# Router logits and the first pair's gather placed between the halves of the output projection, on rows before their norm

## The chip, the cores and the metric

One core of a Trainium2 chip. The metric is device time in microseconds (us) of one execution; lower is better. The engines are TensorE (PE; its weight loads are listed as PEld), VectorE (DVE), ScalarE (ACT), GpSimd (POOL) and SyncE (SP), which here only issues transfers. POOL issues transfers too.

## The reference, cut to what matters

One decoder layer for 320 tokens: a prompt of 256 and 8 sequences of 8 new tokens ("the sample"). Two recurrent mixers, a gated merge, an output projection, then a mixture of 32 experts of which each token takes 4:

```python
merged = sigmoid(gate_a) * (o_a @ w_up_a) + sigmoid(gate_b) * (o_b @ w_up_b)
x = x + merged @ w_o
h2 = _rms(x, norm2_w)                       # x * rsqrt(mean(x*x) + eps) * norm2_w
logits = h2 @ w_router + b_router
top_v, top_e = top_k(logits, 4)
gates = softmax(top_v)
# each chosen expert e: (clip(up) + 1) * swish(min(gate, 7)) @ w_down[e], weighted by its gate
x = x + sum over the four experts
y = _rms(x, norm_f_w)
```

All is float32. An expert has 8 MB of gate and up weights and 4 MB of down weights; all 32 are read, 403 MB.

## The kernel before, in words

Tokens lie in three tiles: tile 0 and tile 1 are the prompt's 128 rows each, tile 2 the sample's 64, kept as 128 half rows of 512 columns (`xs`). `TILE_ORDER` is 2, 0, 1.

**The ring.** `ring` has 12 slots of 1 MB. In the layer, five slots take the panels of the input and up projections in turn (`MIX`), and the four after them (5 to 8) the output matrix `w_o` (`WO`, L432); `merged`, the input of the output projection, lies in the ring behind these (L173). In the expert loop the ring is six chunks of 2 MB (`chunk`): four of gate and up weights, two of down weights. It thus holds one expert. SP loads chunks 1 and 0 of expert 0 when the last up projections are done (L438) and chunks 2 to 5 when the last product with `w_o`, named `wo11`, is (L441). After that, `load_expert` (L447) fetches chunk c of the next expert as soon as TensorE has used chunk c of this one.

**Order of work.** Each engine runs its own list, written out by hand; engines meet at semaphores. The eight PSUM banks are handed out by a list of names, `psum_order`: the i-th name gets bank i mod 8. `take` waits until the bank's last user has emptied it, `done` signals that it is full, `free` that it is emptied.

**The stretch of the change** on TensorE (L1000 to L1133): product `wo2` (sample tile; L628), `wo00` (tile 0, left half of the columns; L967), the sum of squares of the sample (L1010), `wo01`, the turning of the gate and up biases (L1015), the turning of the sample's normed rows `h2s` (L978), `wo10` (tile 1), the sample's logits (L998), `wo11`, then turning (L983) and logits (L998) of tile 0 and tile 1, then for each tile the slot of every token in its experts (`place`, L1034 and L1037: running counts by a triangular matmul), the counts (L1062), the gather of the rows of the first two experts (`gather_part`, L1047: a one-hot matrix `Psel` times `h2`), its turning (`turn_tokens`, L1054), the turning of the gates (L1129), the reading of the loop count, and the loop, which begins with `gate_up` (L628).

DVE adds the products to the residual rows (L1770, L1801), scales them by the inverse root and the norm weights (`norm_rows`, L1779, L1782), finds the four best experts (`top4`, L1787 to L1793: one compare and add for each of the four), turns slots into one-hot matrices (L1817, L1818, L1827), and computes counts (L1832 to L1836) and gates (L1839, L1841). ACT squares rows for the norm (L1189, L1381), evicts turned rows (L1389, L1393), takes the exponentials (L1396, L1397), and evicts gathered and turned tokens (L1422, L1426). POOL loads the norm weights when the last up projection is done (L537 to L542), six transfers that `s_late` counts with two of bias matrices, and TensorE waits for `s_late` ahead of the biases' turn.

The loop takes two experts in a turn and gathers the rows of the next two meanwhile.

Of the kernel before, what the change touches and what calls it, by code (L numbers as in the profile page):

```python
# [16 lines left out]
ALU = mybir.AluOpType  # L17
ACT = mybir.ActivationFunctionType
AX_X = mybir.AxisListType.X

D = 1024
# [41 lines left out]

def psum_order():
# [34 lines left out]
    o += ["wo2", "wo00", "x2s", "wo01", "bgu", "hT2", "wo10", "lg2", "wo11", "hT00", "hT01", "lg0", "hT10", "hT11", "lg1"]  # L99
    o += [f"sl{s}" for s in TILE_ORDER] + ["cnt", "wT"]  # L100
# [3 lines left out]
PSUM_USE = {name: (i % 8, i // 8) for i, name in enumerate(psum_order())}  # L104


def build(nc, x_prompt, x_sample, state_gdn, state_gdn_conv, state_gla, norm1_w, w_in, conv_w, a_log, dt_bias,
# [3 lines left out]
    with ExitStack() as ctx:  # L111
# [61 lines left out]
        merged = flat(ring, (MIX + WO) * 2048, (KD, TOK))  # L173
        gate_b23 = flat(ring, W1 + 3072, (2, TOK))
# [27 lines left out]
        rows = sb("rows", [64, 128])  # L202
        cols = sb("cols", [128, 64])
# [26 lines left out]
        slot1 = sb("slot1", [128, 3, EXPERTS])  # L230
# [20 lines left out]
        iota = sb("iota", [128, SLOTS])  # L251

# [40 lines left out]
        s_cst, xl_ready, xg2_ready, gbr_ready = sem("cst_in"), sem("xl_ready"), sem("xg2_ready"), sem("gbr_ready")  # L293
# [97 lines left out]

        def chunk(c):
            return ring[:, 4096 * c:4096 * c + 4096]
# [5 lines left out]
        def _(sp):  # L399
# [7 lines left out]
            sp.dma_start(rows[58:60, :], gla_gk_b[0].rearrange("(k p) -> k p", p=128)).then_inc(s_rows, 16)  # L407
            sp.dma_start(cst_rows, state_gdn_conv[0].rearrange("b w c -> (b w) c")).then_inc(s_cst, 16)
# [61 lines left out]
        def _(pool):  # L470
# [27 lines left out]
            for g in range(2, 4):  # L498
# [5 lines left out]
                           allow_small_or_imprecise_dtypes=True))  # L504
            step(pool.memset(ab[:, :, :], 0.0), consts)
# [7 lines left out]

            freed(pool, "tail2")
# [31 lines left out]
            step(pool.memset(y_sl, 0.0))  # L546
            step(pool.memset(GTs, 0.0), gtr_done)
# [3 lines left out]
        def _(pe):  # L551
# [30 lines left out]
            for s in range(3):  # L582
                if s == 1:
                    pe.wait_ge(s_rows, 16 * 5)
                    o = take("cols")
                    done(pe.transpose(o[:, 0:60], rows[0:60, :], ident[0:60, 0:60]), "cols")
# [375 lines left out]
            def wo(s, f):  # L962
                n, a = TILE_N[s], TILE_0[s]
                o = take(f"wo{s}{f}")
                for k in range(KD):
                    c = D * (k % 2) + 512 * f
                    mm = pe.matmul(o[0:n, :], merged[:, k, a:a + n], slot(MIX + k // 2)[:, c:c + 512],  # L967
                                   start=(k == 0), stop=(k == KD - 1))
                done(mm, f"wo{s}{f}")

            def turn_h2(s):

                n = TILE_N[s]
                pe.wait_ge(h2_ready, 1 + TILE_ORDER.index(s))
                if s == 2:
                    o = p3(take("hT2"), 4, 128)
                    for k in range(4):
                        mm = pe.transpose(o[:, k, :], h2s[:, 128 * k:128 * k + 128], ident[:, :])  # L978
                    done(mm, "hT2")
                for f in range(2 if s < 2 else 0):  # L980
                    o = p3(take(f"hT{s}{f}"), 4, 128)
                    for k in range(4):
                        mm = pe.transpose(o[:, k, 0:n], h2[0:n, s, 512 * f + 128 * k:512 * f + 128 * k + 128],  # L983
                                          ident[0:n, 0:n])
                    done(mm, f"hT{s}{f}")

            def logits(s):

                n, a = TILE_N[s], TILE_0[s]
                if s < 2:  # L990
                    freed(pe, f"hT{s}1")
                    freed(pe, f"hT{s}0")
                else:
                    freed(pe, "hT2")
                o = take(f"lg{s}")
                for k in range(KD):
# [3 lines left out]
                done(mm, f"lg{s}")  # L1000

            o = take("wo2")
            for k in range(KD):
                mm = halves(o, merged[:, k, PROMPT:TOK], slot(MIX + k // 2)[:, D * (k % 2):D * (k % 2) + D], k == 0,
                            k == KD - 1)
            done(mm, "wo2")
            wo(0, 0)
            pe.wait_ge(x2_sum, 1)
            o = take("x2s")
            done(pe.matmul(o[:, 0:1], pairs[:, :], ss[:, 5:6], start=True, stop=True), "x2s")  # L1010
            wo(0, 1)
            pe.wait_ge(s_late, 128)
            o = take("bgu")
            for j in range(4):
                mm = pe.transpose(o[:, 128 * j:128 * j + 128], b_raw[:, j:512:4], ident[:, :])  # L1015
            done(mm, "bgu")
            turn_h2(2)
            wo(1, 0)
            pe.wait_ge(s_misc, 64)
            logits(2)  # L1020
            wo(1, 1)
            turn_h2(0)
            logits(0)
            turn_h2(1)
            logits(1)

            def place(s):
# [10 lines left out]
                done(mm, f"sl{s}")  # L1038

# [16 lines left out]

            place(2)
            place(0)
            place(1)
            o = take("cnt")  # L1060
            for i, s in enumerate(TILE_ORDER):
                mm = pe.matmul(o[:, 0:EXPERTS], ones[0:TILE_N[s], :], msk[0:TILE_N[s], s, :], start=(i == 0), stop=(i == 2))  # L1062
            done(mm, "cnt")
# [44 lines left out]
            def emptied(banks):  # L1108

                for b in banks:  # L1110
                    pe.wait_ge(pfree[b], max(u for nm, (bb, u) in PSUM_USE.items() if bb == b and nm != "wT") + 1)
# [12 lines left out]
            pe.wait_ge(gate_ready, 3)  # L1124
            assert PSUM_USE["wT"][0] not in (0, 1, 6, 7)
            o = take("wT")
            for s in range(3):
                n, a = TILE_N[s], TILE_0[s]
                mm = pe.transpose(o[0:EXPERTS, a:a + n], gate_all[0:n, s, 0:EXPERTS], ident[0:n, 0:n])  # L1129
            done(mm, "wT")  # L1130
# [804 lines left out]
```

## Time and profile before

| | |
|---|---|
| median of 3 runs | 1383.34 us (1382.59 to 1384.22) |
| profiled execution, its own time | 1385.51 us |
| its span, first to last instruction | 1383.4 us |
| TensorE busy | 1300.4 us, 94% of the span |
| DVE, ACT, POOL busy | 433.2, 296.3, 32.4 us |
| mean granted TensorE clock | 0.983 |
| bytes moved by transfers | 447.71 MB, mean 324 GB/s |

Times in rows are microseconds from the span's start, "mean ns" is one instruction's duration, x the number of instructions, and L12 is line 12 of the kernel. What stands after an arrow `<-` in a wait is what ended it. A granted clock of 1.00 is 2.4 GHz, 0.50 is 1.2 GHz. Matmuls are pipelined, so that their durations overlap; the pace is read from starts, or from the chain of waits.

### The profile page before, as it was taken

Reading aid. Unit: us, or ns where it says so; the run is one execution under the profiler, and the core shown is the slowest. Engines: PE = TensorE matmul, PEld = TensorE weight load, DVE = VectorE, ACT = ScalarE, POOL = GpSimd, SP = SyncE. Lnnn points to the kernel's source line nnn. Section 1 sums busy time; section 2 is a strip of 40 time slices with the busy share of each in tenths; the row PEclk is TensorE's granted clock in tenths of the full one; section 3 lists DMA queues with packets and bytes.
Section 4 is the critical chain, followed back from the end, with each engine's and each line's share of the span. In section 5 each row is a group of like instructions: output and inputs, shape, how many; then the busy total and the mean of one; then the engine's idle time right before and its main releaser. Section 6 shows DMA issues by size and latency. Waiting matters only on the chain.

```text
span 1383.4 us, 15693 instructions
## 1 busy us (share of the span) xinstructions
PE 1300.4 (94%) x5861; PEld 613.2 (44%) x5861; DVE 433.2 (31%) x806; ACT 296.3 (21%) x530; POOL 32.4 (2%) x71
## 2 busy tenths in 40 slices
PE   7999989989999999999999999999999999999996
PEld 5777678746545333333333333333333333333332
DVE  3536566273123231223212133121232212232123
ACT  2374542220022022021120111111021110211102
POOL 5000000001000000000000000000000000000000
PEclk9999989999997999999999999999999999999999
DMA  9522200217536999999999999999999999999993
GB/s 276 170 88 70 92 31 1 69 61 244 198 122 256 417 429 428 428 428 429 428 429 428 429 428 429 428 429 429 429 428 429 428 429 428 428 429 428 429 428 137
DMA packets 61833, 447.71 MB, mean 324 GB/s; under 512 B 7597, under 2 KB 30201, under 8 KB 37228
## 3 DMA queue, kind: packets, MB, share of 16 engines
q1 hardware_dynamic: 59820, 440.34, 77.1%
q0 software_dynamic: 1984, 6.98, 1.5%
q8 instruction: 18, 0.29, 0.1%
q14 instruction: 11, 0.09, 0.0%
HBM read 442.29 MB, written 5.02 MB: 323 GB/s over the span
## 4 chain that ended last, share of the span: by engine, by line
PE 46%; DMA 46%; DVE 5%; ACT 1%; issue 1%; SPq 0%; DVEq 0%; ACTq 0%
DMA ring<-in_w_gate_up_dram 46%; PE bank L628 18%; PE bank L577 14%; PE bank L967 2%; PE bank L1047 2%; PE bank L831 1%; PE bank L642 1%; PE bank L843 1%; PE bank L839 1%; PE bank L998 0%; PE bank L619 0%; PE bank L1054 0%; PE bank L1076 0%; PE bank L677 0%; PE bank L1096 0%
## 5 line engine op out<-in xcount | busy, mean ns | idle before, releaser
L628 PE MATMUL bank<-ring,zgb 128*64 128x512 f32 x2560 | 565.7, 596 | 46.1 <-DMA ring<-in_w_gate_up_dram 36.9
L628 PEld LDWEIGHTS bank<-ring,zgb 128*64 128x64 f32 x2560 | 179.5, 137 | 429.0 <-issue 329.7
L1880 DVE COPY zgb<-bank 128x512 f32<-128x512 f32 x32 | 22.1, 692 | 637.0 <-PE bank L628 637.0
L577 PE MATMUL bank<-hTb,ring 128*128 128x320 f32 x640 | 179.5, 439 | 1.3 <-DVE hTb L1498 1.3
L577 PEld LDWEIGHTS bank<-hTb,ring 128*128 128x128 f32 x640 | 121.9, 192 | 53.8 <-issue 4.7
L628 PE MATMUL bank<-ring,cv 128*64 128x512 f32 x512 | 116.9, 598 | 0.0
L1431 ACT COPY zgb<-bank 128x512 f32<-128x512 f32 x32 | 18.8, 587 | 419.5 <-PE bank L628 419.5
L1047 PE MATMUL bank<-h2b,Sl 128*128 128x512 f32 (+1 forms) x204 | 86.0, 630 | 0.0
L1441 ACT COPY hTb<-bank 64x512 f32<-64x512 f32 x64 | 37.1, 580 | 197.4 <-PE bank L628 196.4
L1076 PE MATMUL bank<-hTb 128*128 128x512 f32 x136 | 68.2, 606 | 0.0
L1855 DVE TENSOR_TENSOR xbuf<-xbuf,bank 128x512 f32<-128x512 f32 x85 | 58.4, 687 | 20.1 <-PE bank L628 11.2
L628 PEld LDWEIGHTS bank<-ring,cv 128*64 128x64 f32 x512 | 33.9, 136 | 58.7 <-issue 54.8
L1096 PEld LDWEIGHTS bank<-ident,zgb 128*128 128x128 f32 x256 | 39.4, 204 | 34.8 <-ACT zgb L1431 19.5
L1047 PEld LDWEIGHTS bank<-h2b,Sl 128*128 128x128 f32 (+1 forms) x204 | 29.8, 197 | 32.6 <-issue 32.5
L1096 PE MATMUL bank<-ident,zgb 128*128 128x128 f32 x256 | 42.3, 288 | 0.0
L1422 ACT COPY h2b<-bank 128x512 f32<-128x512 f32 x34 | 19.9, 586 | 66.7 <-PE bank L1047 66.7
L1426 ACT COPY zgb<-bank 128x512 f32<-128x512 f32 x34 | 19.9, 586 | 58.7 <-PE bank L1054 58.2
L1076 PEld LDWEIGHTS bank<-hTb 128*128 128x128 f32 x136 | 22.3, 193 | 22.9 <-issue 22.9
L1435 ACT ACTIVATE Gc<-qb 128x512 f32<-128x512 f32 x32 | 20.2, 632 | 43.4 <-DVE qb L1891 42.9
L1827 DVE TENSOR_TENSOR Sl<-iota,vTM 128x192 f32<-128x192 f32 x66 | 23.6, 358 | 18.0 <-DVE cv L1896 8.1
L1889 DVE TENSOR_TENSOR qb<-bank,Sg 128x512 f32<-128x512 f32 x32 | 22.1, 692 | 21.7 <-PE bank L1096 18.3
L967 PE MATMUL bank<-ring 128*128 128x512 f32 x64 | 28.4, 597 | 0.0
(388 smaller groups left out, 984.6 us busy)
## 6 DMA issues: line engine op xcount, KB each, us to landing
ring<-in_w_gate_up_dram SPq DMA_DIRECT2D x128, 2048.0 KB, 23.6
ring<-in_w_down_dram SPq DMA_DIRECT2D x64, 2048.0 KB, 20.6
ring<-in_w_in_dram SPq DMA_DIRECT2D x22, 1024.0 KB, 5.2
ring<-in_w_o_dram SPq DMA_DIRECT2D x4, 1024.0 KB, 12.4
ring<-in_w_up_a_dram SPq DMA_DIRECT2D x2, 1024.0 KB, 4.9
ring<-in_w_up_b_dram SPq DMA_DIRECT2D x2, 1024.0 KB, 5.0
out_dram<-Sg POOLq DMA_DIRECT2D x1, 2048.0 KB, 13.1
xbuf<-in_x_prompt_dram SPq DMA_DIRECT2D x2, 512.0 KB, 3.9
```

Of the source, the lines that this page charges most:

```text
L577: mm = pe.matmul(o[0:m, 0:TOK], w[:, k, c0:c0 + m], rhs[:, k, :], start=(k == 0), stop=(k == kk - 1))
L628: mm = pe.matmul(o[64 * f:64 * f + 64, 0:width], lhs, w[f] if isinstance(w, list) else w[:, width * f:width * f + width], start=start, sto ...
L967: mm = pe.matmul(o[0:n, :], merged[:, k, a:a + n], slot(MIX + k // 2)[:, c:c + 512], start=(k == 0), stop=(k == KD - 1))
L1047: return pe.matmul(o[:, :], lhs, rhs, start=(s == TILE_ORDER[0]), stop=(s == TILE_ORDER[-1]))
L1076: mm = pe.matmul(bank[SC[j]][:, :], GTs[:, TILE_0[s]:TILE_0[s] + 128], y_sl[:, 512 * f:512 * f + 512], start=True, stop=True)
L1096: mm = pe.transpose(bank[FMB[q]][:, 128 * j:128 * j + 128], pre[:, q, j:512:4], ident[:, :])
L1435: link(A(sbuf_[:, :, :, :], gbuf[:, :, :, :], ACT.Sigmoid, scale=ALPHA), sg_ready, n * 2 + (x + 1))
L1441: ins = nc.scalar.copy(y_sl[SLOTS * x:SLOTS * x + SLOTS, 512 * f:512 * f + 512], bank[DN[x]][64 * f:64 * f + 64, :])
L1827: return TTo(dst[:, :, SLOTS * x:SLOTS * x + SLOTS], mid(iota[:, :], 3), c, ALU.is_equal)
L1855: link(TTo(v, v, bank[SC[j]][:, :], ALU.add), acc_done, n * 5 + i)
L1880: link(V.tensor_copy(pre[:, 1, :], bank[PRE[1]][:, :]), pre_done[1], n * 2 + (x + 1))
L1889: inner(TTo(dst[:, :, :, :], src, bias, ALU.add))
```

## The change

- **Routing on rows before the norm.** Logits are taken from the residual rows themselves; the router matrix is scaled once by the norm weights (as columns, read with the small rows at the start), and the inverse root comes in when DVE adds the router's bias. The square sums of a prompt tile are taken by halves of its columns.
- **By halves, between the products.** The turning, the logits, the slots and the counts of tiles 2 and 0 stand between the products of the output projection and between the halves of those of tile 1; those of tile 1 as far as its rows are there.
- **The first pair's gather** is made per tile, and turned: the residual rows are the stationary operand and the one-hot matrix, scaled by the inverse root, the moving one. DVE's eviction applies the norm weights. The first `gather_part` and `turn_tokens`, their evictions on ACT and their waits are gone; those in the loop stay, and their semaphore counts shift.
- **`top4`** compares all four experts in one instruction and sums them in a second.
- **The output matrix** goes into the last four slots, `merged` into `h2b` (prompt and sample apart, so two adds); chunk 3 of expert 0 is issued behind the output matrix, chunk 2 with chunks 1 and 0, chunks 4 and 5 behind `wo11`.
- **Moved:** the scaled rows `h2` behind the gates; POOL's clearing of two tiles no longer stands in front of ACT's exponentials; DVE's wait for all output transfers stands ahead of the first product's add.

The diff, cut:

```diff
-        merged = flat(ring, (MIX + WO) * 2048, (KD, TOK))
+        merged = flat(h2b, 0, (2, KD, 128))
+        merged_s = flat(h2b, 2 * D, (KD, 64))
...
+            sp.dma_start(rows[60:68, :], norm2_w[0].rearrange("(k p) -> k p", p=128)).then_inc(s_rows, 16)
...
-                sp.dma_start(slot(MIX + k).rearrange("p (k n) -> p k n", k=2), src).then_inc(wfull[MIX + k], 16)
+                sp.dma_start(wo_slot(k).rearrange("p (k n) -> p k n", k=2), src).then_inc(wfull[MIX + k], 16)
+            sp.dma_start(chunk(3), expert_chunk(0, 3)).then_inc(e_full[3], 16)
...
-                if i % MIX in (3, 0):
-                    c = {3: 1, 0: 0}[i % MIX]
+                if i % MIX in (3, 4, 0):
+                    c = {3: 1, 4: 2, 0: 0}[i % MIX]
...
-            for c in range(2, CHUNKS):
+            for c in range(4, CHUNKS):
...
+            pool.dma_start(n2p[:, :].rearrange("p (k i) -> p k i", i=2), norm2_w[0].rearrange("(k p i) -> p k i", p=128, i=2)
+                           ).then_inc(s_n2p, 16)
...
+            def first_tokens(s, f):
+                o = p3(bank[f], 4, 2 * SLOTS)
+                pe.wait_ge(first_ready, TILE_ORDER.index(s) + 1)
+                for k in range(4):
+                    c = 256 * (k // 2) + k % 2
+                    if s < 2:
+                        lhs, rhs = x_tm[:, s, 512 * f + c:512 * f + c + 255:2], Psel[:, s, :]
...
+            wo_part(0, 0, take("wo00"), range(KD))
+            turn_x2(2, 0)
...
+            wo_part(0, 1, take("wo01"), range(KD))
+            pe.wait_ge(s_late, 128)
...
+            pe.wait_ge(wr_ready, 1)
+            logits_part(2, take("lg2"), range(KD))
+            turn_x2(0, 0)
+            turn_x2(0, 1)
+            o = take("wo10")
+            wo_part(1, 0, o, range(4))
             place(2)
+            lg0 = take("lg0")
+            logits_part(0, lg0, range(4))
+            logits_part(0, lg0, range(4, KD))
+            wo_part(1, 0, o, range(4, KD))
             place(0)
+            cnt = take("cnt")
+            count(2, cnt)
+            count(0, cnt)
+            o = take("wo11")
+            wo_part(1, 1, o, range(4))
+            turn_x2(1, 0)
+            wo_part(1, 1, o, range(4, KD))
+            lg1 = take("lg1")
+            logits_part(1, lg1, range(4))
+            turn_x2(1, 1)
...
+            for f in range(2):
+                first_tokens(2, f)
+            logits_part(1, lg1, range(4, KD))
+            for f in range(2):
+                first_tokens(0, f)
             place(1)
+            done(count(1, cnt), "cnt")
+            for f in range(2):
+                first_tokens(1, f).then_inc(xt_full[f], 1)
+            pe.wait_ge(gate_ready, 3)
...
-            emptied((6, 7))
-            pe.wait_ge(p_ready, 1)
-            for f in range(2):
-                gather_part(f, 2)
-            for f in range(2):
-                gather_part(f, 0)
-                gather_part(f, 1).then_inc(g_full[7 - f], 1)
-            emptied(range(6))
-            for f in range(2):
-                pe.wait_ge(xr_done, f + 1)
-                turn_tokens(f)
...
+                step(TTo(merged_s[:, m, :], ga[:, PROMPT:TOK], gb[:, PROMPT:TOK], ALU.add))
+                step(TTo(merged[:, :, m, :], ga, gb, ALU.add), mrg_ready)
...
+            dve.wait_ge(s_misc, 64)
+            step(TTo(wr[:, :, :], wr[:, :, :], last(cols[:, 60:68], EXPERTS), ALU.mult), wr_ready)
...
+            dve.wait_ge(out_sem, 96)
             o = full(dve, "wo2")
             free(TTo(xs, xs, o[:, :], ALU.add), "wo2")
             add_rows("wo00", 0, 0)
+            inverse_rms(2)
             add_rows("wo01", 0, 1)
+            top4(2)
+            inverse_rms(0)
+            first_slots(2)
+            top4(0)
             add_rows("wo10", 1, 0)
+            first_slots(0)
             add_rows("wo11", 1, 1)
+            o = p3(full(dve, "hT11"), 4, 128)
+            free(V.tensor_copy(hT[:, 4:8, 128:256], o), "hT11")
+            inverse_rms(1)
             top4(1)
+            first_slots(1)
...
+            for f in range(2):
+                dve.wait_ge(xt_full[f], 1)
+                step(TTo(xTe[:, 4 * f:4 * f + 4, :], p3(bank[f], 4, 128), last(n2p[:, 4 * f:4 * f + 4], 128), ALU.mult),
+                     xg_done)
+            dve.wait_ge(s_late, 128)
+            for s in range(3):
+                norm_rows(s)
```

## Rows read from the trace of the kernel before

**Rows 1.** Busy time of each engine by stretch (from:to, length, engines).

```profile
core 0: us, PE busy (x) PEld busy (x) DVE busy (x) ACT busy (x) POOL busy (x), PEclk, DMA share, GB/s
...
360.00:371.00 11.00, 11.00 (x43) 7.75 (x42) 0.49 (x1) 0.87 (x2) 0.00 (x0) 1.00 0.00 0
...
431.00:444.00 13.00, 10.63 (x37) 4.42 (x37) 2.51 (x8) 4.25 (x7) 0.00 (x0) 0.80 0.03 10
...
500.00:1340.00 840.00, 798.58 (x3514) 290.21 (x3512) 206.70 (x362) 128.58 (x214) 0.00 (x0) 1.00 1.01 428
```

**Rows 2.** TensorE's waits over the whole span (us in total, times, longest).

```profile
PE bank L628 <- DMA ring<-in_w_gate_up_dram: 36.9, 38, 1.2
```

**Rows 3.** Timeline of the SP queue's issues (start, us, line, count).

```profile
371.75 0.82 SPq L438 DMA_DIRECT2D ring<-in_w_gate_up_dram  x2
...
410.01 0.81 SPq L441 DMA_DIRECT2D ring<-in_w_gate_up_dram  x2
...
443.79 10.62 SPq L447 DMA_DIRECT2D ring<-in_w_gate_up_dram  x4
```

**Rows 4.** The chain that ended last, 368 to 460 us (start, us, what).

```profile
372.84 7.09 PE bank L628 x32
...
402.92 7.08 PE bank L967 x16
...
413.65 1.97 PE bank L998 x16
...
418.04 3.64 PE bank L998 x16
...
426.54 7.75 PE bank L1047 x12
...
436.88 1.35 issue
...
438.24 15.65 PE bank L628 x64
```

**Rows 5.** Busy time and granted clock in stretches of 5 us.

```profile
410.00:415.00 5.00, 2.20 (x20) 1.96 (x19) 2.14 (x3) 2.62 (x5) 0.00 (x0) 1.00 0.82 272
...
420.00:425.00 5.00, 4.93 (x23) 4.41 (x23) 2.82 (x14) 1.79 (x2) 1.33 (x2) 0.50 1.00 429
...
425.00:430.00 5.00, 4.99 (x12) 2.69 (x13) 3.84 (x18) 2.67 (x10) 0.00 (x0) 0.50 1.00 429
...
440.00:445.00 5.00, 5.00 (x18) 1.51 (x16) 0.00 (x0) 0.00 (x0) 0.00 (x0) 0.71 0.18 33
```

**Rows 6.** Groups of DVE instructions by line, 365 to 440 us (busy, mean ns).

```profile
L1770 DVE TENSOR_TENSOR xbuf<-xbuf,bank 128x512 f32<-128x512 f32 x4 | 2.8, 688 | 18.7 <-PE bank L967 18.7
...
L1764 DVE TENSOR_TENSOR ring<-Gc,ring 128x320 f32<-128x320 f32 x1 | 0.5, 493 | 0.0
...
L1787 DVE TENSOR_TENSOR lgt<-bank,brt 128x32 f32<-128x32 f32 x3 | 0.6, 192 | 5.9 <-PE bank L998 5.9
```

**Rows 7.** Timeline of TensorE: transposes, one slot matmul, gates turned.

```profile
409.82 1.04 PE L983 MATMUL bank<-ident,h2b 128*128 128x128 f32 x8
...
422.50 0.63 PE L1037 MATMUL bank<-msk,triu 128*128 128x32 f32 x2
...
435.58 0.54 PE L1129 MATMUL bank<-ident,vTM 128*32 128x128 f32 x3
```

**Rows 8.** Timeline of DVE: its wait for POOL's last norm load.

```profile
389.65 0.17 DVE L1777 RECIPROCAL rs<-rs 128x1 f32<-128x1 f32 x1 [1.86 <-DMA xbuf<-in_norm_f_w_dram]
```

**Rows 9.** Timeline: SP's issue before the first panel, TensorE's first projection.

```profile
4.18 0.30 SPq L408 DMA_DIRECT2D zgb<-in_state_gdn_conv_dram  x1
...
14.14 7.28 PE L577 MATMUL bank<-hTb,ring 128*128 128x320 f32 x16 [1.25 <-DVE hTb L1498]
```

**Rows 10.** Group of weight loads that turn the gathered rows, 365 to 440 us.

```profile
L1054 PEld LDWEIGHTS bank<-ident,h2b 128*128 128x128 f32 x8 | 1.2, 206 | 0.9 <-issue 0.5 <-ACT h2b L1422 0.5
```

More of the change, by code:

```diff
@@ L987, in logits, with wo_part @@
[L987 to L996, printed above, removed]
+            def wo_part(s, f, o, ks):
+                for k in ks:
+                    c = D * (k % 2) + 512 * f
+                    mm = pe.matmul(o[:, :], merged[:, s, k, :], wo_slot(k // 2)[:, c:c + 512],
+                                   start=(k == 0), stop=(k == KD - 1))
+                if KD - 1 in ks:
+                    done(mm, f"wo{s}{f}")
@@ new lines, in turn_x2, with logits_part @@
+            def turn_x2(s, f):
+                freed(pe, "wo2" if s == 2 else f"wo{s}{f}")
+                nm = "hT2" if s == 2 else f"hT{s}{f}"
+                x = xs if s == 2 else x_tm[:, s, 512 * f:512 * f + 512]
+                o = p3(take(nm), 4, 128)
+                for k in range(4):
+                    mm = pe.transpose(o[:, k, :], x[:, 128 * k:128 * k + 128], ident[:, :])
+                done(mm, nm)
+            def logits_part(s, o, ks):
+                n, a = TILE_N[s], TILE_0[s]
+                freed(pe, "hT2" if s == 2 else f"hT{s}{ks[0] // 4}")
+                for k in ks:
@@ L999, in logits @@
                                        stop=(k == KD - 1))
[L1000 to L1025, printed above, removed]
+                if KD - 1 in ks:
+                    done(mm, f"lg{s}")
             def place(s):
@@ L1038, in place, with count @@
                 done(mm, f"sl{s}")
+            def count(s, o):
+                return pe.matmul(o[:, 0:EXPERTS], ones[0:TILE_N[s], :], msk[0:TILE_N[s], s, :], start=(s == TILE_ORDER[0]),
+                                 stop=(s == TILE_ORDER[-1]))
+            def first_tokens(s, f):
+                o = p3(bank[f], 4, 2 * SLOTS)
+                pe.wait_ge(first_ready, TILE_ORDER.index(s) + 1)
+                for k in range(4):
+                    c = 256 * (k // 2) + k % 2
+                    if s < 2:
+                        lhs, rhs = x_tm[:, s, 512 * f + c:512 * f + c + 255:2], Psel[:, s, :]
+                    else:
+                        u = slice(64 * f, 64 * f + 64)
+                        lhs, rhs = xs[u, c:c + 255:2], Psel[u, 2, :]
+                    mm = pe.matmul(o[:, k, :], lhs, rhs, start=(s == TILE_ORDER[0] and k == 0),
+                                   stop=(s == TILE_ORDER[-1]), skip_group_check=True)
+                return mm
             def gather_part(f, s):
@@ L1055, in turn_tokens @@
                 mm.then_inc(xt_full[f], 1)
+            o = take("wo2")
+            for k in range(KD):
+                mm = halves(o, merged_s[:, k, :], wo_slot(k // 2)[:, D * (k % 2):D * (k % 2) + D], k == 0, k == KD - 1)
+            done(mm, "wo2")
+            wo_part(0, 0, take("wo00"), range(KD))
+            turn_x2(2, 0)
+            pe.wait_ge(x2_sum, 1)
+            o = take("x2s")
+            done(pe.matmul(o[:, 0:1], pairs[:, :], ss[:, 5:6], start=True, stop=True), "x2s")
+            wo_part(0, 1, take("wo01"), range(KD))
@@ L1057, in _ @@
+            pe.wait_ge(s_late, 128)
+            o = take("bgu")
+            for j in range(4):
+                mm = pe.transpose(o[:, 128 * j:128 * j + 128], b_raw[:, j:512:4], ident[:, :])
+            done(mm, "bgu")
+            pe.wait_ge(wr_ready, 1)
[4 more added lines that the diff above has]
+            wo_part(1, 0, o, range(4))
             place(2)
+            lg0 = take("lg0")
+            logits_part(0, lg0, range(4))
@@ L1390, in take_h2 @@
                     free(nc.scalar.copy(hT[:, 4:8, a:a + 64], o[:, :, 64:128]), "hT2")
-                for f in range(2 if s < 2 else 0):
+                else:
                     o = p3(full(act, f"hT{s}{f}"), 4, 128)
@@ L1791, in top4 @@
                 step(V.tensor_copy(rif[:, s, :], ri8[:, s, :]))
-                for k in range(TOP):
-                    step(STT(out=msk[:, s, :], in0=iota[:, 0:EXPERTS], scalar=rif[:, s, k:k + 1], in1=msk[:, s, :],
-                             op0=ALU.is_equal, op1=ALU.add), mask_ready if k == TOP - 1 else None)
-            step(V.memset(msk[:, :, :], 0.0))
+                step(TTo(chosen[:, :, :], mid(iota[:, 0:EXPERTS], TOP), last(rif[:, s, 0:TOP], EXPERTS), ALU.is_equal))
+                step(V.reduce_sum(msk[:, s, :], chosen[:, :, :].rearrange("p k e -> p e k"), AX_X), mask_ready)
@@ L1842, in _ @@
                      gate_ready)
+            for f in range(2):
[3 more added lines that the diff above has]
+            dve.wait_ge(s_late, 128)
+            for s in range(3):
+                norm_rows(s)
             for s in range(3):
```

198 lines of the change are left out of this document (94 added, 104 removed).

## The prediction, made before the changed kernel ran

> **What bounds the kernel now.** I read the stage table first, for the bytes moved in each stretch [rows 1]. The kernel has two parts. Up to about 444 us the layer itself runs, with transfers off and on. Then the expert weights stream without a pause: 428 GB/s over 840 us, while TensorE, busy 798.58 of 840, has gaps. The list of TensorE's waits agrees: 36.9 us for expert weights [rows 2]. So from the restart of the weight stream on, the end is set by the transfers, and an engine made faster inside the loop would gain nothing.
>
> What sets the restart? The ring holds one expert. It is filled, and then chunk 0 of the next expert may only be fetched when the loop's first matmuls have used chunk 0 of the first. The SP queue's rows show it [rows 3]: two chunks issued at 371.8, the others at 410.0, and then nothing until 443.79, 5.55 us after the loop's first matmul at 438.24. The hole is plain: 10 GB/s from 431 to 444 [rows 1]. **Each microsecond by which the restart comes earlier is a microsecond off the end**, since the 31 experts of 6 chunks behind it run at the stream's own rate.
>
> Then the chain of waits in front of 438.24 [rows 4]. The five output products run from 372.84 to 410.00 with the bias turn, the sample tile's turn and its logits among them. Behind them stand 28 us in which TensorE does little work: logits of the prompt tiles (1.97 and 3.64 us for the same 16 matmuls), slots, a gather of 12 matmuls of 512 columns (7.75 us), its eviction and turning, then 1.35 us for reading the loop count. The clock rows show why the same logits cost twice: the granted clock is 0.50 (1.2 of 2.4 GHz) from 420 to 430 [rows 5].
>
> **The change part by part, against the profiled execution.**
>
> *Merged rows.* The last of eight adds becomes two on the path, 64 and 256 columns in place of 320 (0.493 us [rows 6]): between nothing and one more add of 0.49; by columns only the second instruction's fixed part is added, so 0.2.
>
> *Moved between the products.* TensorE now issues there 12 transposes (8 take 1.04 us [rows 7], so 1.6), tile 0's logits (1.97 [rows 4]), and 12 small matmuls for slots and counts (2 took 0.63 at the low clock [rows 7], so 0.16 each at the high one: 1.9). The last product ends at 410.00 + 0.2 + 5.5 = **415.7**. The waits in front of them are covered: half of each product (3.5 us) stands between a turn and its logits, and between logits and slots, where DVE needs some eight steps of 0.2 us (0.192 for 32 columns [rows 6]).
>
> *Behind the last product.* Tile 1's logits 1.97, four transposes 0.5, first gather of the sample tile and tile 0. The new gather yields turned rows at once: 8 matmul instructions of 128 columns for each tile and half, 48 in all. No row shows it. The lower bound is the 0.123 us that one instruction of tile 0's logits takes (128 weight columns loaded each time), the upper one 0.23, tile 1's logits at the low clock [rows 4]; I take 0.123, as it is the same weight load. Four groups: 3.9, so 422.1. Slots and count of tile 1, 8 x 0.16, of which 1.0 lie ahead of DVE; two compares there, 0.6; then tile 1's gather, 2.0: **425.7**. On DVE, 12 small steps (2.4 us) from 423.7 to 426.1 give counts and gates, TensorE turns the gates (0.54 [rows 7]), reads the count (1.35 [rows 4]) and starts the loop at **428.1**. DVE's two scaling evictions (0.69 each [rows 6]) end at 427.5, just hidden; if they weren't, they would cost 1.4.
>
> *Removed.* Two compares before the gather, the 7.75 us gather, two evictions, two turns, two more evictions, the wait for the eviction of the gates. They are the difference to 438.24: **10.1 us**.
>
> *Queues.* SP issues chunk 3 after the output matrix and chunk 2 with chunks 1 and 0 at 371.8; no transfer runs from 360 to 371 [rows 1]. Behind the last product two chunks are left, 4.2 MB or 9.8 us at 428 GB/s, landing at about 427. With four left they would have ended near 437, behind the loop's start, so this part is needed, though alone it gains nothing. POOL's loads of norm weights now share the engines with three chunks, not two. They landed by 389.65 [rows 8]; 2.1 MB more at 428 GB/s is 4.9 us, so 394.6 at the latest. TensorE waits for them before the bias turn, at 394.5: nothing to 0.5 us. The extra small load in front of SP's first panel costs about 0.3 us of issue [rows 9]; TensorE's first projection started behind DVE, not a panel, so 0, and 0.3 if that cover is gone. POOL's extra ramp and load lie in its idle time. DVE's wait for the output transfers moves ahead of all it does for the products, where the first product's add would queue behind it; nothing was in flight from 360 to 371 [rows 1], so they have ended. TensorE's new wait for the scaled router matrix is for one early DVE multiply. The three scaled row tiles (2560 columns, 3.5 us at 0.69 for 512 [rows 6]) go behind the gates; only gathers inside the loop read them, and DVE has nothing to do for the loop's products until the first 64 matmuls end (15.65 us [rows 4]). Uncovered, they would cost those 3.5.
>
> *The restart.* It came 5.55 us after the loop's start because the clock was low in part of that stretch (0.71 from 440 to 445 [rows 5]). Chunks are freed 3.54 us apart afterwards (10.62 for three steps [rows 3]), so a high clock would give 3.54. Before 438.24 TensorE had stood idle for the count; it will again. I take 5.55: restart at 433.7 instead of 443.79.
>
> *Sum.* 10.1 us, less 0.6 for the norm loads and for waits that rows can't show: 9.5. The profiled execution took 1385.51 us (span 1383.4), so 1376.0 in its terms. It stands 2.2 above the median of 1383.34; the median becomes **1373.8, say 1374.0**, within 1372 to 1376.
>
> **A rule against the trace.** From 420 to 425 TensorE was busy 4.93 of 5 us and from 425 to 430 4.99 of 5, at a granted clock of 0.50 all the while [rows 5]; its work was small matmuls, then the gather. The Trainium skill (TensorE: Matmul & The Clock Gate, "What's actually happening") says that throttling is the default state and activity releases it. By that alone, the new order, with hardly a gap, would keep 2.4 GHz throughout; these rows disagree, for a busy engine stayed at 1.2. By the rule the sum would be rival 1's time, by the rows the forecast's.
>
> **Rivals.**
> 1. *The clock stays high to the end of the first chunk.* Then restart is 428.1 + 3.54 = 431.6, 12.1 us earlier: 1371.2. For it: gaps in the new order are of 0.5 to 1.4 us only. Against it: the 1.35 us wait was followed by 0.71 [rows 5]. The rule of the Trainium skill above would give this time.
> 2. *The clock falls among the small matmuls*, as it did behind 415. If it falls at 419, 6.8 us of TensorE's work ahead of the loop doubles, of which 1 hides in waits: start at 433.9, restart 5.55 to 7.1 later, 4.3 to 2.8 us gained: 1379 to 1380.5. A fall at 422 gives 1376.5. For it: 415 to 430 at 0.50. Against it: before that fall TensorE was busy only 2.20 of 5 us [rows 5], which the new order avoids.
> 3. *Slower: the gather's weight loads.* Its stationary operand takes every second column of the rows. If that made a load slow, 48 of them stand in the chain. It decides where 48 x (x - 0.123) exceeds 12.9 us (10.1 and the 0.2%): at 0.39 us for each. At 0.45 it costs 15.7 us, the loop starts at 443.8, and the time is 1389. Against it: turning the gathered rows reads the same stride, at 0.206 us a load, overlapped [rows 10].
> 4. *Nothing measurable:* an early fall of the clock (rival 2) and the norm loads late by over 1 us together. The gain sinks under 2.8 us: 1381 to 1383.
>
> **How the numbers follow.** My forecast 0.42, rival 1 0.20, rival 2 0.26, rival 4 0.08, rival 3 0.04. The bound of 0.2% (2.8 us) is about what a measurement of this kernel can tell from no change. Forecast and rivals 1 and 2 are faster: 0.88. The range runs from rival 1 with 0.7 us for the clock and other bounds, 1370.5, to rival 2's far end, 1380.5; it leaves out rivals 3 and 4 and some edges.
>
> **What would show it.** Right: last product ending near 415.7, loop's first matmul near 428, SP's restart near 433.7, no idle TensorE above 1 us except at the count, and the loop from there on as before. The clock rows between 415 and 435 tell forecast, rival 1 and rival 2 apart. Wrong: weight loads of the new gather above 0.3 us; TensorE idle before the bias turn; a stream that pauses again after its restart, or a restart that moved without the end moving.

## The result, and the profile after

The changed kernel takes 1375.0 us in the median of 5 runs (1372.88 to 1375.77), beside 1382.59 for the kernel before on the same chip: ratio 0.9939, 95% interval 0.9927 to 0.995. On record stood 1374.0, within 1370.5 to 1380.5, and 0.88 for faster.

The profiled execution is the quickest of the five: it took 1372.88 us, span 1371.1, against a span of 1383.4 before. First its stretches, in the columns of [rows 1].

```profile
core 0: us, PE busy (x) PEld busy (x) DVE busy (x) ACT busy (x) POOL busy (x), PEclk, DMA share, GB/s
360.00:371.00 11.00, 10.84 (x41) 7.32 (x39) 0.54 (x2) 0.87 (x2) 0.00 (x0) 1.00 0.01 4
431.00:444.00 13.00, 13.00 (x61) 5.28 (x58) 5.38 (x15) 0.58 (x1) 0.00 (x0) 1.00 0.94 373
500.00:1340.00 840.00, 796.13 (x3502) 288.27 (x3502) 203.76 (x358) 127.38 (x213) 0.00 (x0) 1.00 1.01 428
```

The stretch from 431 to 444, a hole of 10 GB/s before, now moves 373 GB/s; the long stretch runs at 428 as it did. The SP queue's issues show the restart itself, the last row here (443.79 in [rows 3]):

```profile
370.93 1.29 SPq L463 DMA_DIRECT2D ring<-in_w_gate_up_dram  x3
414.84 0.81 SPq L466 DMA_DIRECT2D ring<-in_w_down_dram  x2
430.94 10.62 SPq L472 DMA_DIRECT2D ring<-in_w_gate_up_dram  x4
```

The restart is 12.85 us earlier and the span 12.3 shorter. From the restart to the end it is 940.2 us, 939.6 before: the gain at the restart reaches the end nearly one for one.

The medians are only 7.6 us apart: the profiled execution of the kernel before lies 2.9 above its median, this one 2.1 below. So the pair of profiles is counted from the first matmul of the output products, 372.84 in [rows 4] and here

```profile
372.21 7.09 PE L657 MATMUL bank<-ring,h2b 128*64 128x512 f32 x32 [1.37 <-DVE h2b L1812]
```

From there to the loop's first matmul (427.08, shown below) it is 54.9 us, 65.4 before. That is 10.5 of the 12.3; 0.6 lie ahead of the products, 1.7 between the loop's start and the restart, and 0.6 are lost behind it.

The chain that ended last (start, us, what) shows how the loop came to start early; it answers to [rows 4].

```profile
373.80 20.32 DMA xbuf<-in_norm_f_w_dram
394.12 0.04 issue
394.16 0.75 PE bank L1084 x4
...
411.38 3.44 PE bank L995 x8
414.81 0.81 PE bank L1016 x8
415.62 0.04 issue
415.66 0.66 PE bank L1007 x4
416.32 1.72 PE bank L1050 x16
418.04 1.01 PE bank L1016 x8
419.04 1.97 PE bank L1050 x16
...
427.08 13.95 PE bank L657 x64
```

The last product (L995) ends at 414.8. Behind it stand halves of tile 1's logits (L1016), four transposes (L1007) and the first gathers (L1050), one after another. The loop's first 64 matmuls start at 427.08 (438.24 before) and take 13.95 us, not 15.65. TensorE's timeline has its only waits between the last product and the loop in brackets:

```profile
422.74 2.15 PE L1050 MATMUL bank<-Sl,xbuf 128*128 128x128 f32 x16 [0.61 <-DVE Sl L1849]
425.49 0.55 PE L1123 MATMUL bank<-ident,vTM 128*32 128x128 f32 x3 [0.60 <-DVE vTM L1896]
427.08 5.37 PE L657 MATMUL bank<-ring,zgb 128*64 128x512 f32 x24 [1.04 <-DVE zgb L1900]
```

And the stretches of 5 us, where [rows 5] had a granted clock of 0.50:

```profile
415.00:420.00 5.00, 4.96 (x43) 4.56 (x43) 2.21 (x8) 3.73 (x10) 0.89 (x1) 1.00 0.85 295
420.00:425.00 5.00, 4.28 (x33) 3.82 (x31) 3.76 (x18) 1.75 (x4) 0.43 (x2) 1.00 1.00 421
425.00:430.00 5.00, 3.47 (x17) 1.30 (x19) 4.79 (x7) 1.90 (x3) 0.00 (x0) 1.00 0.30 128
```

The clock is 1.00 (2.4 GHz) throughout. So the earlier start has two possible sources, less work behind the last product and the same work at twice the clock, and the experiments were made to part them.

### The profile page after: what moved, and what is told of

Read it like the earlier page. It is cut to its first block, busy times and chain, and to the rows that moved or that the text cites. A ratio compares the mean times of both kernels' runs of the same rounds, so it can differ in the third digit from the quotient of the medians.

```text
span 1371.1 us, 15699 instructions
## 1 busy us (share of the span) xinstructions
PE 1290.5 (94%) x5889; PEld 608.9 (44%) x5889; DVE 437.7 (32%) x815; ACT 294.3 (21%) x531; POOL 33.2 (2%) x73
## 4 chain that ended last, share of the span: by engine, by line
DMA 48%; PE 45%; DVE 5%; issue 1%; ACT 1%; POOL 0%; SPq 0%; DVEq 0%; ACTq 0%
DMA ring<-in_w_gate_up_dram 46%; PE bank L657 17%; PE bank L606 14%; DMA xbuf<-in_norm_f_w_dram 1%; PE bank L1061 1%; PE bank L860 1%; PE bank L671 1%; PE bank L995 1%; PE bank L872 1%; PE bank L868 1%; PE bank L648 1%; PE bank L1068 0%; PE bank L1140 0%; PE bank L640 0%; PE bank L1016 0%
## 5 line engine op out<-in xcount | busy, mean ns | idle before, releaser
L657 PEld LDWEIGHTS bank<-ring,zgb 128*64 128x64 f32 x2560 | 179.2, 137 | 426.9 <-issue 327.3
L1061 PE MATMUL bank<-h2b,Sl 128*128 128x512 f32 (+1 forms) x192 | 78.3, 609 | 0.0
L1061 PEld LDWEIGHTS bank<-h2b,Sl 128*128 128x128 f32 (+1 forms) x192 | 27.0, 190 | 28.3 <-issue 28.3
L995 PE MATMUL bank<-ring,h2b 128*128 128x512 f32 x64 | 28.8, 598 | 0.0
```

The lines of the kernel that those rows point to most:

```text
L657: mm = pe.matmul(o[64 * f:64 * f + 64, 0:width], lhs, w[f] if isinstance(w, list) else w[:, width * f:width * f + width], start=start, sto ...
L995: mm = pe.matmul(o[:, :], merged[:, s, k, :], wo_slot(k // 2)[:, c:c + 512], start=(k == 0), stop=(k == KD - 1))
L1061: return pe.matmul(o[:, :], lhs, rhs, start=(s == TILE_ORDER[0]), stop=(s == TILE_ORDER[-1]))
```

## The experiments

Every ratio below is to the kernel before in the same session. Its median was 1382.41 us beside after_again, late_chunks, behind and old_gather, 1382.16 beside behind_fill, before_fill, delay and fill, and 1383.07 beside fill_again and fill_early.

**1. The change once more (after_again).** No edit.

> The changed kernel once more, for a second trace beside the kernels it is compared with. Theory 1 (the end follows the restart of the weight stream, and the restart follows the loop's first matmul): median 1372 to 1376, first matmul at 427 to 428.5, SP's first issue in the loop 3.5 to 5.6 us behind it, and whatever the time is, span minus restart is 940 us within 1. Theory 2 (what was gained is the clock alone): the same time, but an execution whose clock falls between 415 and 430 would start the loop near 432 and lose most of the gain.

1373.69 us (1372.01 to 1376.2), ratio 0.993 (0.9917 to 0.9943). Its profiled execution took 1376.2, and it isn't like the first: the loop starts at 428.07, and the clock falls right behind the start (stretches of 5 us, then the restart on SP's queue).

```profile
425.00:430.00 5.00, 3.36 (x19) 1.57 (x19) 4.69 (x10) 1.90 (x3) 0.00 (x0) 0.89 0.50 213
430.00:435.00 5.00, 5.00 (x22) 1.61 (x20) 3.28 (x11) 0.00 (x0) 0.00 (x0) 0.77 0.19 36
```

```profile
433.62 10.62 SPq L472 DMA_DIRECT2D ring<-in_w_gate_up_dram  x4
```

From start to restart it is 5.55 us here and 3.86 in the first profile. The same kernel does both, behind the same wait of 1.0 us; that accounts for 1.7 of the 4 us over which its runs spread.

**2. Four chunks left behind the last product (late_chunks)**, as before the change.

```diff
-            sp.dma_start(chunk(3), expert_chunk(0, 3)).then_inc(e_full[3], 16)
...
-                if i % MIX in (3, 4, 0):
-                    c = {3: 1, 4: 2, 0: 0}[i % MIX]
+                if i % MIX in (3, 0):
+                    c = {3: 1, 0: 0}[i % MIX]
...
-            for c in range(4, CHUNKS):
+            for c in range(2, CHUNKS):
```

> Chunks 2 and 3 of the first expert go back behind the last output product; all else as changed. Theory 1: the loop starts at 427 as before, but four chunks behind 414.8 keep the engines busy for 19.6 us, to about 435.7, and the next expert's chunk 0, issued at 431, queues behind them; of the 9.8 us of extra transfer 4.4 fall into what is now a hole, so the time rises by 5.4 us over the changed kernel, to about 1380. Rival: the early chunks are hidden anyway and the time stays at 1375.

1374.49 us (1372.81 to 1376.3), ratio 0.994 (0.9927 to 0.9953). The 5 us that I expected are not there. SP's issues and the stream behind the restart:

```profile
413.99 0.80 SPq L465 DMA_DIRECT2D ring<-in_w_gate_up_dram  x2
414.84 1.30 SPq L465 DMA_DIRECT2D ring<-in_w_down_dram  x2
431.82 10.62 SPq L471 DMA_DIRECT2D ring<-in_w_gate_up_dram  x4
```

```profile
430.00:435.00 5.00, 5.00 (x26) 1.76 (x24) 2.93 (x10) 0.00 (x0) 0.00 (x0) 1.00 1.02 436
```

The queue is indeed still full when the next expert's chunk 0 is issued at 431.82. But the last bytes of the first expert land at 436.0, and of the next expert's last chunk at 465.6, against 463.8 in the changed kernel, whose restart was 0.9 earlier. The change's hole was short anyway: after the issue at 430.94 the stream moved 213 GB/s between 432 and 434 and 410 between 434 and 436. So the two chunks fetched early are worth about 1 us by the landings. The medians (0.8 apart, intervals overlapping) don't tell even that from nothing, nor does the time from the restart to the end, 940.3 us as in the other profiles. The clock fell in this execution too, 5.55 us from start to restart.

**3. The new work behind the last product (behind).** The two products of tile 1 run whole first, then the turns, logits, slots and gathers in the changed kernel's own form; only the sample's turn and logits stay ahead, where they were before the change. DVE's adds and ACT's first squares for tile 1 move with the products.

```diff
+            wo_part(1, 0, take("wo10"), range(KD))
+            wo_part(1, 1, take("wo11"), range(KD))
...
-            o = take("wo10")
-            wo_part(1, 0, o, range(4))
...
-            wo_part(1, 0, o, range(4, KD))
...
-            o = take("wo11")
-            wo_part(1, 1, o, range(4))
...
-            wo_part(1, 1, o, range(4, KD))
...
```

> Turning, logits, slots and counts of tile 0 and the first turn of tile 1 go behind the last output product, which ends 5 us earlier. The gather per tile, the chunks and all instructions stay. Theory 1: the same TensorE work with its waits uncovered: some 3 us of waits for DVE and ACT appear behind the last product, the loop starts at 430 to 431 at the high clock, 1378. Theory 2: 8 us of small matmuls in a row let the clock fall to 0.5 before the loop starts, the loop starts at 433 to 436 and the time is 1380 to 1384. Rival: order is worth nothing, 1375.

1382.11 us (1380.39 to 1383.89, 12 runs), ratio 0.9995 (0.9986 to 1.0004): the whole gain is gone, though not one matmul was added. Its stretches of 5 us:

```profile
415.00:420.00 5.00, 4.18 (x19) 3.68 (x19) 0.88 (x4) 2.49 (x5) 0.00 (x0) 0.50 1.00 429
420.00:425.00 5.00, 5.00 (x27) 4.45 (x26) 0.86 (x2) 1.82 (x7) 0.00 (x0) 0.50 0.24 98
425.00:430.00 5.00, 5.00 (x28) 4.76 (x28) 2.01 (x10) 1.76 (x4) 1.33 (x2) 0.68 0.00 2
```

TensorE waits 1.5 us for tile 0's mask and 0.8 us for an eviction, and from 414.6 to 428.2 the clock is 1.2 GHz, with the engine busy 5.00 of 5 us from 420 on. The chain has the price of that: the sample's 16 gather instructions take 3.02 us here and 1.72 in the changed kernel, the half of tile 1's logits behind them 1.84 and 1.01.

```profile
420.95 3.02 PE bank L1050 x16
423.97 1.84 PE bank L1016 x8
```

The loop starts at 435.02 and the restart is at 440.57: the 5.55 us of a low clock in the first chunk again. So what the move between the products is worth is either the work it hides or the clock it keeps. Experiment 4 parts these.

**4. The same with the clock held (behind_fill).** Four matmuls whose results nobody reads are added to behind: one ahead of tile 0's logits, two in the wait for its mask, one in a wait for a turn. The diff shows the two.

```diff
...
+            for _ in range(2):
+                pe.matmul(bank[7][:, 0:512], ones[:, :], oAb[:, 0:512], start=True, stop=True)
...
```

> The kernel with routing behind the products, with four such matmuls added (one ahead of tile 0's logits, two in the wait for its mask, one in the wait for tile 1's first turned half). Clock theory: the fall at 414.6 goes, the loop starts at 429 to 430 instead of 435.0, and the time is 1375.5 to 1377.5. Order theory: the waits behind the last product are what costs, the start stays at 434 to 436 and the time at 1382.

1375.87 us (1373.81 to 1377.76), ratio 0.9953 (0.994 to 0.9967). **More work, and some 6 us less time** (6.2 by the medians of the two sessions, 5.8 by the ratios). From 410 to past the restart the clock never falls; two of its stretches:

```profile
415.00:420.00 5.00, 5.00 (x38) 3.95 (x38) 1.91 (x6) 3.21 (x6) 0.00 (x0) 1.00 0.99 426
420.00:425.00 5.00, 4.75 (x39) 4.35 (x36) 2.27 (x11) 2.27 (x9) 1.32 (x2) 1.00 0.15 61
```

The loop starts at 429.73, 5.3 us before behind's start (0.5 of it was there at the last product's end), and the restart follows 3.85 us later. The order by itself, work hidden beside products, is worth what is left to the changed kernel. From the products' first matmul (371.98 here) to the loop's it is 57.8 us against 54.9, so 2.9 us at most: the four matmuls take 3.7 us, and the waits that they fill came to 2.5 in behind.

**5. The kernel before with the clock held (before_fill).** Eight unread matmuls in the waits of the old order, three and two ahead of logits, two ahead of the slots, one ahead of the loop.

```diff
+            def spare(name, n):
+                b, u = PSUM_USE[name]
+                pe.wait_ge(pfree[b], u)
+                for _ in range(n):
+                    pe.matmul(bank[b][:, :], ones[:, :], oAb[:, 0:512], start=True, stop=True)
...
+            spare("lg0", 3)
```

> The kernel before, with eight matmuls of 512 columns added whose results nobody reads, 0.88 us each at the high clock, put where TensorE waited behind the last product (3 ahead of tile 0's logits, 2 ahead of tile 1's, 2 ahead of tile 1's slots, 1 ahead of the count). Clock theory (a good part of what the change gained is the clock): it holds 1.00 at least to 425, tile 1's logits take 1.97 instead of 3.64 us and the gather 5.3 instead of 7.75, the loop starts at 431 to 434 and the time is 1376 to 1379, with more work. Order theory (the chain of steps itself was too long): the clock changes little, the loop starts at 438 or later, 1382 to 1385.

1378.8 us (1377.85 to 1381.26, 11 runs), ratio 0.9976 (0.9967 to 0.9985): 3.4 us gained without any of the change. In the timeline tile 1's logits take 1.87 us where [rows 4] had 3.64, and the old gather 6.41 where it had 7.75. The loop starts at 432.82, 5.4 us earlier than in the profile before; but 2.4 of that were there when the last product ended (407.6 against 410.0), so 3.0 are the fillers' gain ahead of the loop. The restart follows 3.85 us behind the start, not 5.55.

```profile
415.67 1.87 PE L998 MATMUL bank<-wr,hTb 128*128 128x32 f32 x16
...
422.59 6.41 PE L1057 MATMUL bank<-h2b,Sl 64*128 64x512 f32 x12 [0.55 <-DVE Sl L1839]
...
432.82 2.37 PE L628 MATMUL bank<-ring,zgb 128*64 128x512 f32 x10
```

```profile
415.00:420.00 5.00, 5.00 (x30) 3.34 (x29) 2.58 (x13) 0.93 (x1) 1.32 (x2) 1.00 1.01 433
420.00:425.00 5.00, 4.45 (x19) 2.69 (x19) 3.88 (x20) 3.53 (x11) 0.00 (x0) 0.85 1.02 433
```

The clock still falls from 423.5 to 426.9, so a little more may be won from the kernel before in this way; no run shows it.

**6. The old first gather in the new order (old_gather).** Rows are scaled, gathered by 12 matmuls of 512 columns and turned, as in the kernel before; DVE's scaling goes back ahead of tile 1's routing with it.

```diff
-            for f in range(2):
-                first_tokens(2, f)
...
+            for f in range(2):
+                gather_part(f, 2)
+            for f in range(2):
+                gather_part(f, 0)
+                gather_part(f, 1).then_inc(g_full[7 - f], 1)
...
+                turn_tokens(f)
```

> The first pair is gathered as rows behind all slots and then turned, as in the kernel before; the routing stays between the halves of the products and the chunks stay early. Theory 1: 12 matmuls of 0.44 us, two evictions, two turns and two evictions more stand in the chain (8.2 us) in place of the last tile's gather, its waits and two evictions (4 us): loop start at 431 to 432 at the high clock, 1379 to 1380. Theory 2: the wait for the compares lets the clock fall and the gather takes 7.8 us as it did: start at 434 to 435, 1382 to 1384.

1378.92 us (1376.38 to 1380.37), ratio 0.9966 (0.9954 to 0.9978), 5.2 us over the changed kernel in the same session. The loop starts at 434.49, where theory 2 put it; the time is theory 1's, since the first chunk then runs at the high clock (3.85 us from start to restart). TensorE now waits 2.2 us for tile 1's mask, and the clock is low around that wait:

```profile
420.00:425.00 5.00, 2.13 (x8) 1.80 (x8) 4.24 (x15) 2.47 (x9) 1.33 (x2) 0.50 1.03 441
```

The wait is not for the gather's matmuls. The old gather reads scaled rows, and here DVE's scaling (L1836), 3.35 us in three pieces, stands in the chain ahead of that mask:

```profile
417.12 0.76 DVE h2b L1836
...
418.63 1.30 DVE h2b L1836
...
420.15 1.29 DVE h2b L1836
...
423.24 0.65 PE bank L1031 x2
```

So the new gather, with the scaling that it lets DVE do later, is worth some 5 us here, the clock that falls without them among them; this run can't split the three.

**7. A later loop (delay).** Eight unread matmuls straight ahead of the loop.

> The changed kernel with eight such matmuls of 512 columns between the gates' turn and the loop, 7.0 us of which some 1 us lies in the wait for the count. Restart theory: first matmul 6 us later, at 433 to 434, restart 6 us later, and the time 6 us longer, 1379.5 to 1380.5, one for one. Rival (a start made later is caught up inside the loop, where TensorE waits 37 us for weights): 1374 to 1376.

1379.95 us (1377.37 to 1380.1), ratio 0.9975 (0.9964 to 0.9985). They took 7.06 us, 1.0 of it in the wait that stood there, the loop started at 433.9 and the restart came at 437.73, from where 940.6 us led to the end. Beside the first profile of the change, which had the high clock in the first chunk too, start and restart are 6.8 us later and the span is 7.2 longer. The median is 6.3 us over after_again's of the other session, 5.3 over that of all eleven runs of the change. This shows the rule that the whole sum rests on from the other side: a later start of the loop goes nearly one for one into the time.

**8. The change with its last waits filled (fill, fill_again).** Three unread matmuls in the waits of 0.61, 0.60 and 1.04 us shown above.

```diff
...
+            for _ in range(1):
+                pe.matmul(bank[7][:, 0:256], ones[:, :], oAb[:, 0:256], start=True, stop=True)
...
```

> The changed kernel with three such matmuls in its own last waits (two of 256 columns ahead of the last gather and of the gates' turn, one of 512 while the count is read). Clock theory: the low stretch that began at 428.9 in one execution and was absent in another goes in most, and the median falls by 1 to 2 us, to 1372 to 1373. Rival: the clock falls there for other reasons, or the added matmuls stand in the way: 1374 to 1376.

> The kernel fill once more beside fill_early, for the comparison of the two on one chip: 1372.5 to 1374.5, the loop's first matmul between 426 and 428.5.

1373.47 us (1372.34 to 1374.54), ratio 0.9936 (0.9923 to 0.9949), and 1372.16 us (1370.45 to 1375.14), ratio 0.9922 (0.9907 to 0.9936). In both profiles the clock stays at 1.00 past the restart and the loop starts at 426.50 and 426.09:

```profile
425.00:430.00 5.00, 4.97 (x23) 1.65 (x23) 4.79 (x7) 1.90 (x3) 0.00 (x0) 1.00 0.17 72
```

Over eleven runs each the median is 1373.5 with them and 1374.7 without. The intervals overlap, and the runs come from several sessions: a gain of about 1 us is possible, but not shown.

**9. Three earlier waits filled as well (fill_early).** Elsewhere the clock falls too: in fill from 189 to 196, near 290 and near 306. Seven unread matmuls of 128 columns go into the wait ahead of each.

```diff
+            spare("t20", 7)
...
+                    if m == 2:
+                        spare("ss20", 7)
...
+                    spare("ua0", 7)
```

> The kernel fill with 21 more matmuls of 128 columns whose results nobody reads, seven in each of three earlier waits of TensorE (2.1 us ahead of 189.1, 2.0 us ahead of 287.7, 2.4 us ahead of 303.2 in fill). Theory 1 (the clock falls after each such wait, and spare matmuls hold it): the low stretches near 190 to 196, 288 to 292 and 305 to 309 go; each was 3.4 us or more at 1.2 GHz, so the loop's first matmul comes 2 to 5 us earlier than fill's 426.5, between 421.5 and 424.5, and the time is 1368.5 to 1371.5. Theory 2 (VectorE sets the pace of these stretches, so that a quicker TensorE only waits longer): the low stretches go too, but the start stays within 1 us of 426.5 and the time at 1372.5 to 1374.5.

1375.17 us (1372.65 to 1376.01), ratio 0.9935 (0.9922 to 0.9948): no gain over fill, and in the profile the loop starts at 430.17, 4.1 us later than in fill_again. The low stretch near 190 shrank (some 3.4 us at the low clock, 6.8 in fill, by their rows of 5 us), but the two later ones did not go; they moved. Two rows of fill_early:

```profile
296.00:300.00 4.00, 4.00 (x10) 2.10 (x7) 3.79 (x7) 0.00 (x0) 0.00 (x0) 0.50 0.00 0
...
315.00:320.00 5.00, 5.00 (x14) 3.24 (x13) 4.76 (x8) 0.00 (x0) 1.72 (x1) 0.66 0.04 3
```

Up to 312 us VectorE sets the pace (busy 3.79 of 4 us in the first of these rows), so a slow TensorE costs little there: the group ahead of the long run of projections starts at 312.60, in fill_again at 311.79. Behind it TensorE sets the pace, and there the moved stretch is paid for. The first group of the run in fill_early, then in fill_again:

```profile
314.66 4.11 PE L606 MATMUL bank<-oAb,ring 128*128 128x320 f32 x8
```

```profile
313.85 2.42 PE L606 MATMUL bank<-oAb,ring 128*128 128x320 f32 x8
```

With 1.55 us for a norm load, 0.8 + 1.7 + 1.55 is the 4.1. The load took 21.6 us from issue to landing where it took 20.3 in the change; no run ties that to the fillers, so 1.55 of the 4.1 may be this execution's alone. My first theory is wrong; the second, that VectorE sets the pace, holds for the stretches up to 312, but it also forecast that the low stretches go and the start stays within 1 us of 426.5, and that failed.

## Why the prediction was right

**The restart decides.** Right. From restart to end it is 939.2 to 940.9 us in all twelve profiled executions, with restarts from 429.94 to 443.79.

**The last product at 415.7.** 414.8 in one profile, 415.8 in the other; the difference lies ahead of the products, which began at 372.21 and 373.16. From their first matmul to the last product's end it is 42.6 us in both, 37.2 before: 5.4 more, where the sum had 5.5. The parts agree: tile 0's logits 1.90 (1.97 forecast), the twelve transposes between products 1.02 and 0.44 (1.6), slots and counts 1.58 (1.9), the two adds in place of one 0.65 us, not 0.49 (0.2 more); as groups of DVE instructions:

```profile
L1812 DVE TENSOR_TENSOR h2b<-Gc,h2b 128x256 f32<-128x256 f32 x1 | 0.4, 424 | 0.0
L1810 DVE TENSOR_TENSOR h2b<-Gc,h2b 128x64 f32<-128x64 f32 x1 | 0.2, 225 | 0.0
```

**The new gather at 0.123 us an instruction.** Measured 1.72, 1.97 and 2.15 us for 16: 0.108 to 0.134. That is the lower bound, and the reason given (the same weight load as in the logits) stands: its loads take 193 and 196 ns on average, the logits' 191. The slower rival of loads above 0.39 us falls.

**The loop's start at 428.1.** 427.08 and 428.07, both 54.9 us behind the products' first matmul; 65.4 before makes 10.5, where the sum had 10.1 and the 0.2 of the merged rows. The scaling evictions, costed as just hidden, are not quite: TensorE waits 1.04 us for them; in return only 0.19 us of the 1.35 for the count stand in the chain behind them, the rest lies beside that wait.

**The norm loads, 0 to 0.5 us.** They landed at 394.1, the bound was 394.6, and TensorE waited 0.3. In fill_early, where the last load took 1.3 us longer, it waited 1.55: the cover was as thin as the sum had it, and the wait can pass its 0.5.

**Restart 5.55 us after the start, or 3.54.** Both came. The second profile is the forecast within 0.1 us (428.07 and 433.62 against 428.1 and 433.7). The first is rival 1, whose step from start to restart was mis-sized by 0.3: 3.86 us at the high clock, where I took 3.54, the pace of the chunks behind. It isn't one case or the other for this kernel but one or the other for each execution, and the forecast's 1374.0 lies between their times.

**From the profile to the median.** The sum forecast 1376.0 for a profiled execution, and the second took 1376.2. The 2.2 us taken off for the median are not derived: no row shows where the profile of before lost them, and before_fill, with the same code up to there, starts its products 2.4 us earlier (370.43). That the same 2.2 nearly holds for the changed kernel, one of whose two profiles has the quicker restart, is in part luck.

**The rule against the trace.** The rows of before, TensorE busy 4.93 to 4.99 of 5 us at 0.50, seemed to speak against the Trainium skill (TensorE: Matmul & The Clock Gate, "What's actually happening"), by which activity releases the throttle. behind shows the same again, busy 5.00 of 5 at 0.50 from 420 to 425. Yet where the waits ahead were short or filled, the clock was 1.00 from 415 to 425 (both profiles of the change, fill, behind_fill); why the work behind a longer wait stays at 1.2 GHz, no run shows. Of the two profiles of the change one agrees with what I drew from the page, 2.4 GHz to the end of the first chunk, and one does not; a chance of 0.20 for it was too small.

**What failed.** The step "with four left they would have ended near 437, behind the loop's start, so this part is needed". They ended at 436.0, as worked out; the conclusion was wrong. I held the landing against the loop's start, but the first expert's chunks are used one after another: its last isn't wanted until several steps of 3.5 us later, and TensorE waits for no chunk before 480 us in late_chunks. What the four chunks delay is only the head of the next expert's fetch, by the 4.2 us that the queue is still full behind the restart, and in that place the changed kernel has a slow beginning of its own (213 GB/s up to 434). Worth about 1 us at most, in place of the 5 us that I still put on record for the run. The sum had no term for this part, so the time did not suffer from it.

The other weakness is in "Removed": 10.1 us as one sum of instructions taken away, at the durations that they had. Those were in good part durations at 1.2 GHz (0.50 from 420 to 430 [rows 5]). The medians by two edits show what that sum holds (in us, from several sessions; the last row over the eleven runs of each):

```
                                waits as they are   waits filled
kernel before                        1382.4            1378.8
new work behind the last product     1382.1            1375.9
new work between the products        1374.7            1373.5
```

With the waits filled, the new gather and routing give 2.9 us and the place between the products 2.4. With the waits as they are, the first gives 0.3 and the second 7.4. The split is rough: in before_fill the clock still falls for 3.4 us, and each row has other fillers, which cost something themselves. But 7.4 against 2.4 is clear: most of what the move between the products brings is a clock that doesn't fall, and the number came out right because the forecast had costed every moved part at the high clock. That this was a condition, and which part of the change met it, stood only in rival 2; behind is that rival made to happen.

## What to carry to other kernels

Ahead of a stream of transfers, find the instruction that frees the first buffer: its time goes into the end one for one, and a late transfer counts only against the moment when its data is used. Before a chain of small matmuls is shortened, read the granted clock along it: where it runs at 1.2 GHz, more may be won from the wait ahead of it than from its instructions, and a few unread matmuls in that wait are a cheap trial. Ask first whether TensorE sets the pace there: where it didn't, in fill_early, such matmuls gained nothing, and the low stretch moved behind them into dearer work.

## What the runs showed that I had not expected

Four matmuls that compute nothing, in waits of up to 1.5 us, took some 6 us off a kernel of 1382. And once the clock had fallen it stayed at 1.2 GHz for 13.6 us (414.6 to 428.2 in behind), through small matmuls that kept TensorE busy 4.18 and then 5.00 of 5 us.

The time from the loop's start to the restart has two values in all profiles: 3.85 to 3.86 us where the clock stays high, 5.55 where it falls in the first chunk, nothing between. The same kernel gives one or the other behind the same wait of 1.0 us, and so do behind (low) and behind_fill (high) behind 1.07; what decides it in an execution stays open.
